# Two edits in a two-block network kernel on one core: 24 one-column sums spread over three weight blocks, and the first group of the retention stage reordered

## The chip, the cores and the metric

The kernel runs on one core of one Trainium2 chip. The metric is device time in microseconds, the median of several executions; a profile of one execution gives a span and every instruction in it. TensorE is called PE here (PEld is its weight load), VectorE DVE, ScalarE ACT, GpSimd POOL, and SP is the engine whose queue issues all transfers.

## The reference

Two models are run one after the other on x, 512 tokens by 1024 features, two layers each.

```python
# first block, layer l of 2
cond = silu(c) @ w_ada[l] + b_ada[l]            # 3 * 1024 columns
shift, scale, gate_raw = split(cond, 3)
h = x * (1 + scale) + shift
proj = h @ w_in[l]                              # HGRN2, RWKV7 and gate columns
...
x = layer_norm(DN_ALPHA * x + (1 + gate_raw) * out, ln_g[l], ln_b[l])

# second block: layer 0 is an RG-LRU mixer, layer 1 is retention
h = rms_norm(x, norm_pre[layer])
o = rglru_mixer(h, ...) if layer == 0 else retention_mixer(h, ...)
x = x + rms_norm(o, norm_post[layer])

# retention: u = h @ w_in gives q, k (4 heads of 256), v and a gate (4 heads of 512)
```

What matters here: in layer 0 of the first block, cond of layer 1 is also computed; and retention starts with x = x + rms_norm(o, norm_post[0]) and a projection of rms_norm(x, norm_pre[1]).

## The kernel before, in words

Activations lie transposed: a tile is 128 features by 512 tokens, and x has eight tiles (KT = 8). All large products go through 231 **weight blocks** of 128 x 1024 numbers (512 KB). Each block passes four stations. SP loads it into one of two slots of w_raw (L552, `load_block`; it waits until POOL has finished with the block before in that slot). ACT copies it to w_hi, rounded (L790, `weights(b)`; it waits for the load and until PE has used block b - 2). POOL subtracts the rounded copy from the raw one in two halves into w_lo (L700). PE multiplies it (L2480, `project`, 24 matmuls of 512 columns: for each of eight tiles high x high, low x high, high x low). Activations are split in the same way into act_hi (ACT) and act_lo (DVE). Every engine has its own hand-written program order, and semaphores tie them together; what stands behind a waiting instruction on its engine waits too.

A **group** (L2499, `side_by_side`) is four blocks interleaved so that four output tiles are built at once, input tile by input tile: step k = 0 to 7 takes 12 matmuls with input tile k, and needs act_hi and act_lo of tile k and one half of the w_lo of block k // 2. After step 1, 3, 5 and 7 a block counts as used.

**Conditioning columns.** In layer 0 of the first block `later_step` on DVE adds up w_ada of layer 1 over the features into `later_acc` (3072 sums per partition), and `condition_next` on PE adds over the partitions: 24 matmuls of one column each (L2576; each shows as two records in the trace). It stands after the fourth of the blocks b_hg, ahead of four kk_sum matmuls in full fp32 (L2625) and the fifth block. `ada_gate` (L2614) is a like piece of 8 columns, four blocks earlier.

**Retention's first group.** RET is the first retention block. DVE runs over the eight tiles of x: it scales the old output by post0 and 1/rms (L1431 into slots_sb), adds it to x (L1428 into area_sb, signals x_done), and makes act_lo of the tile before (L1431 into act_lo_sb). ACT makes act_hi (L1326) and the square (L1191) of each tile. Then DVE adds the eight squares, each add waiting for the one before (L1428 into slots_sb, `add_squares`), and PE sums them over the partitions (L3081, job rms_pre1). In PE's order that sum stands ahead of step 7 of the group. ACT turns it into 1/rms (L810, L812 into const_sb, `inverse_root`), which DVE needs only when it takes the outputs.

SP's order at this place is the following. The change leaves it as it is:

```python
            blocks_to(ret + 4)
            sp.wait_ge(S("x_done"), KT * 3)
            sp.dma_start(x_scr[2].rearrange("k p t -> p k t"), xa[:, :, :]).then_inc(S("x_saved"), 16)
            blocks_to(ret + 5)
            sp.wait_ge(S("x_saved"), 48)
```

So all eight tiles of x must be done before SP issues the save of x (2 MB), and the load of block RET + 4, which PE takes right behind the group, is issued behind that save. ACT's order has `weights(RET + 4)` ahead of `inverse_root`.

Of the kernel before, what the change touches and what calls it, by code (L numbers as in the profile page):

```python
# [21 lines left out]
KT = D // P  # L22
# [157 lines left out]
LATER = [(0, k, 2) for k in range(KT)] + [(1, k, part) for k in range(KT) for part in range(3)]  # L180
# [157 lines left out]
def build(nc, shapes):  # L338
    first, pieces, groups = block_plan()
    jobs = job_plan()  # L340
# [8 lines left out]
    with ExitStack() as ctx:  # L349
# [43 lines left out]
        aux = [ctx.enter_context(nc.psum_tensor(f"aux{i}", [P, T], F32)) for i in range(6)] + proj  # L393
# [12 lines left out]
        def S(name):  # L406

            if name not in made:
                made[name] = sem(name)
            return made[name]  # L410

        RW_LAST = [first["hg", l] - 1 for l in range(DEPTH)]
        SPLITS = {("h", 0): 0, ("hg", 0): 8, ("rw", 0): 12, ("merged", 0): 16, ("h", 1): 24, ("hg", 1): 32,
                  ("rw", 1): 36, ("merged", 1): 40, "lru_h": 48, "lru_y": 56, "ret_h": 68, "ret_y": 76}
# [36 lines left out]
        def job_open(eng, name, turn=0):  # L451

            bank, use = jobs(name, turn)
            wait(eng, aux_read[bank], use)
            return aux[bank][:, :]

        def job_full(ins, name):
            return ins.then_inc(aux_full[jobs(name)[0]], 1)
# [290 lines left out]
        LRU, LRU_OUT, RET, RET_OUT = (first[k, 0] for k in ("lru_in", "lru_out", "ret_in", "ret_out"))  # L749
# [29 lines left out]
        def _(act):  # L779
# [3 lines left out]
            def weights(b, turn=0):  # L783


                if b >= blocks:
                    return
                act.wait_ge(raw_in[b % 2], 16 * (b // 2 + 1) + 32 * turn)
                wait(act, block_used, b - 1 + 4 * turn)
                A(w_hi[:, b % 2, :, :].rearrange("p k n -> p (k n)"), w_raw[:, b % 2, :], ACT.Copy)\  # L790
                    .then_inc(hi_ready, 1)
# [29 lines left out]
            for l in range(DEPTH):  # L821
# [47 lines left out]
                for i in range(4):  # L869
                    x = group_ready(act, ("rw", l, i))  # L870
# [17 lines left out]
                for j in range(QT):  # L888
                    scaled(b + 4 + j, 9 + j)
                    x = job_ready(act, ("w_up", l, j))  # L890
                    job_read(A(P1[:, j, :], x, ACT.Sigmoid, bias=V(f"w0{l}", j)), ("w_up", l, j))
                    x = job_ready(act, ("a_up", l, j))
                    job_read(A(P2[:, j, :], x, ACT.Sigmoid, bias=V(f"a0{l}", j)), ("a_up", l, j))
                for j in range(QT):
                    scaled(b + 8 + j, 13 + j)
                    if l:
                        x = job_ready(act, ("v_up", l, j))
# [102 lines left out]
                for t in range(QT):  # L1000
# [4 lines left out]
                    x = job_ready(act, ("v_turn", l, t))  # L1005
# [19 lines left out]
                    x = job_ready(act, ("k_turn", l, t))  # L1025
# [91 lines left out]
                for j in range(QT):  # L1117
                    x = job_ready(act, ("gn_var", l, j))
# [204 lines left out]
            def ret_high(m):  # L1323

                act.wait_ge(S("x_done"), 2 * KT + m + 1)
                A(act_hi[:, m, :], xa[:, m, :], ACT.Copy, scale=V("pre1", m)).then_inc(split_hi, 1)  # L1326

            for m in range(KT):
                ret_high(m)
                own_square(m, xa[:, m, :])  # L1330
                if m in (4, 7):
                    weights(RET + (m + 5) // 4)
            weights(RET + 4)
            inverse_root(RS_RET, "rms_pre1", 1.0 / D, 1e-6, S("rms_rs"))
            weights(RET + 5)
# [87 lines left out]
        def _(dve):  # L1423
# [3 lines left out]
            def tt(out_ap, a, b, op):  # L1427
                return TT(out_ap, a, b, op)  # L1428
# [18 lines left out]
            def add_squares(key, which):  # L1447

                for m in which:
                    dve.wait_ge(sq_ready, SQUARES[key] + m + 1)  # L1450
                    ins = tt(SQ[:, 0, :], SQ[:, 0, :], SQ[:, m, :], ALU.add)
                    if m == which[-1] and m > 5:
                        ins.then_inc(S("squares_added"), 1)
                    else:
                        chain.done(ins)
# [120 lines left out]
            for l in range(DEPTH):  # L1576
# [14 lines left out]
                for i in range(4):  # L1591
                    dve.wait_ge(S("mu_scaled"), 17 * l + i + 1)
                    x = group_ready(dve, ("rw", l, i))
# [12 lines left out]
                if l == 0:  # L1606
                    x = job_ready(dve, "ada_gate")
# [654 lines left out]
            for m in range(KT + 1):  # L2262
                if m < KT:
                    stt(OUT[:, m, :], OUT[:, m, :], V("post0", m), RS, ALU.mult, ALU.mult).then_inc(S("out_scaled"), 1)
                if m:
                    ret_low(m - 1)
                if m < KT:
                    dve.wait_ge(S("out_scaled"), m + 1)
                    tt(xa[:, m, :], xa[:, m, :], OUT[:, m, :], ALU.add).then_inc(S("x_done"), 1)
            dve.wait_ge(S("x_done"), 3 * KT)  # L2270
            dve.sem_inc(split_src, KT)
            add_squares("pre1", (1, 2, 3, 4, 5, 6, 7))

            def rotate(h, n):

# [182 lines left out]
        def _(pe):  # L2458
# [25 lines left out]
            def side_by_side(name, tiles, fresh=None, steps=None, ready=None):  # L2484

                b = groups[name][0]
                for k, t in enumerate(tiles):
                    if steps and k not in steps:
                        continue
                    s = (b + k // 2) % 2  # L2490
                    if ready:
                        ready(k)
                    pe.wait_ge(lo_ready, 2 * b + k + 1)
                    if fresh is not None:
                        pe.wait_ge(split_lo, fresh + k + 1)
                    for i in range(4):
                        bank = aux[jobs(name + (i,))[0]][:, :] if k else job_open(pe, name + (i,))
                        for n, (w, a) in enumerate(((w_hi, act_hi), (w_hi, act_lo), (w_lo, act_hi))):
                            ins = MM(bank, w[:, s, 4 * (k % 2) + i, :], a[:, t, :], start=(k == 0 and n == 0),  # L2499
                                     stop=(k == len(tiles) - 1 and n == 2))  # L2500
                    if k % 2:
                        used(ins)
# [22 lines left out]
            for l in range(DEPTH):  # L2525
# [40 lines left out]
                    if l == 0 and k == 5:  # L2566
                        condition(3)

                def condition_next():

                    pe.wait_ge(S("later_used"), len(LATER))
                    x = job_open(pe, ("ada", 1, 0))
                    for j in range(24):

                        at = j if j > 15 else 8 * (j % 4 // 2) + 2 * (j // 4) + j % 2
                        ins = MM(x[:, at:at + 1], later_acc[:, P * j:P * j + P], C("ones", 0, 1), start=True, stop=True)  # L2576
                    job_full(ins, ("ada", 1, 0))

                if l == 0:
                    stream(0)  # L2580
# [36 lines left out]

                for m in range(4):
                    used(project(b_hg + m))
                if l == 0:  # L2620
                    condition_next()
                for j in range(QT):
                    x = job_open(pe, ("kk_sum", l, j))
                    pe.wait_ge(S("kk_squares"), 4 * l + j + 1)
# [452 lines left out]
            def added_squares(n, job, last):  # L3077

                x = job_open(pe, job)
                pe.wait_ge(S("squares_added"), n)  # L3080
                ins = MM(x, C("ones"), SQ[:, 0, :], start=True, stop=not last)  # L3081
                if last:
                    pe.wait_ge(sq_ready, last)
                    ins = MM(x, C("ones"), SQ[:, 7, :], start=False, stop=True)
                job_full(ins, job)
# [57 lines left out]
            added_squares(2, "rms_post0", SQUARES["post0"] + 8)  # L3143
            keep_busy(("ret_in", 0, 3), 6)

            def ret_root(k):
                if k == 7:
                    added_squares(3, "rms_pre1", 0)

            def ret_block(h, j):  # L3150
                used(project(RET + 12 * h + j))

# [67 lines left out]
                pe.wait_ge(S("ret_squares"), h + 1)  # L3220
                job_full(MM(x, C("ones"), wa[:, :], start=True, stop=True), ("r_var", h))

            side_by_side(("ret_in", 0), range(KT), fresh=SPLITS["ret_h"], ready=ret_root)
            for j in range(4, 11):
                ret_block(0, j)
            turns(0)
# [76 lines left out]
```

## Time and profile before

| | us |
|---|---|
| median of 3 runs | 1815.9 |
| lowest, highest | 1815.09, 1817.47 |
| profiled execution, its own time | 1817.34 |
| its span | 1815.2 |
| PE busy in it | 1744.2 (96%) |
| DVE, ACT, POOL busy | 1149.7, 826.4, 715.2 |

The profiled execution is 1.4 us longer than the median, and 2.1 us of it lie outside its span. PE is busy in 96% of the span, so the time is made up of PE's instructions, the short waits between them, and the clock at which they run. That clock has two levels, full (2.4 GHz) and half (1.2 GHz); its mean over the execution is 0.992 of full.

### The profile page before, as it was taken

Reading aid. Unit: us, or ns where it says so; the run is one execution under the profiler, and the core shown is the slowest. Engines: PE = TensorE matmul, PEld = TensorE weight load, DVE = VectorE, ACT = ScalarE, POOL = GpSimd, SP = SyncE. Lnnn points to the kernel's source line nnn. Section 1 sums busy time; section 2 is a strip of 40 time slices with the busy share of each in tenths; the row PEclk is TensorE's granted clock in tenths of the full one; section 3 lists DMA queues with packets and bytes.
Section 4 is the critical chain, followed back from the end, with each engine's and each line's share of the span. In section 5 each row is a group of like instructions: output and inputs, shape, how many; then the busy total and the mean of one; then the engine's idle time right before and its main releaser. Section 6 shows DMA issues by size and latency. Waiting matters only on the chain. (4 is left out here: it accounts for less than half of the span.)

```text
span 1815.2 us, 32011 instructions
## 1 busy us (share of the span) xinstructions
PE 1744.2 (96%) x12832; PEld 1378.6 (76%) x12832; DVE 1149.7 (63%) x1535; ACT 826.4 (46%) x1233; POOL 715.2 (39%) x488
## 2 busy tenths in 40 slices
PE   7999999989999999999989999999999999999996
PEld 6777777778786767777788785675777888888875
DVE  6677687776567118787775647788637364636454
ACT  3343655544635333655454626476543333324242
POOL 2555443320253435643410452443544433434342
PEclk9999999999999999999999999999999999999998
DMA  9772222210531522222200524321244212222222
GB/s 368 254 254 96 88 88 98 95 42 4 187 104 58 171 80 82 93 91 93 92 31 29 184 95 165 100 70 58 85 136 140 85 65 82 70 70 82 70 95 103
DMA packets 63187, 193.00 MB, mean 106 GB/s; under 512 B 5936, under 2 KB 6192, under 8 KB 62672
## 3 DMA queue, kind: packets, MB, share of 16 engines
q1 hardware_dynamic: 63056, 191.10, 30.7%
q8 instruction: 101, 1.65, 0.4%
q14 instruction: 30, 0.25, 0.0%
HBM read 173.25 MB, written 17.83 MB: 105 GB/s over the span
## 5 line engine op out<-in xcount | busy, mean ns | idle before, releaser
L700 POOL TENSOR_TENSOR w_lo_sb<-w_raw_sb,w_hi_sb 128x512 fp32r<-128x512 f32 x462 | 690.6, 1516 | 981.9 <-ACT w_hi_sb L790 981.8
L2480 PE MATMUL proj<-act_hi_sb,w_hi_sb 128*128 128x512 f32 x1480 | 600.5, 406 | 8.2 <-DVE area_sb L1428 2.3
L2480 PE MATMUL proj<-act_hi_sb,w_lo_sb 128*128 128x512 f32 x1480 | 577.6, 390 | 0.0
L2480 PE MATMUL proj<-act_lo_sb,w_hi_sb 128*128 128x512 f32 x1480 | 576.4, 389 | 0.0
L790 ACT ACTIVATE w_hi_sb<-w_raw_sb 128x1024 fp32r<-128x1024 f32 x231 | 244.3, 1058 | 648.0 <-PE proj L2480 485.1
L2480 PEld LDWEIGHTS proj<-act_hi_sb,w_hi_sb 128*128 128x128 f32 x1480 | 277.9, 188 | 91.3 <-issue 24.4
L2480 PEld LDWEIGHTS proj<-act_lo_sb,w_hi_sb 128*128 128x128 f32 x1480 | 278.2, 188 | 61.7 <-issue 7.7
L2480 PEld LDWEIGHTS proj<-act_hi_sb,w_lo_sb 128*128 128x128 f32 x1480 | 277.8, 188 | 59.7
L2499 PE MATMUL aux<-act_hi_sb,w_hi_sb 128*128 128x512 f32 x336 | 136.9, 407 | 13.7 <-POOL w_lo_sb L700 5.1
L1428 DVE TENSOR_TENSOR area_sb<-area_sb 128x256 f32<-128x256 f32 (+1 forms) x180 | 118.1, 699 | 44.5 <-PE aux L2667 26.6
L2499 PE MATMUL aux<-act_lo_sb,w_hi_sb 128*128 128x512 f32 x336 | 132.2, 393 | 0.0
L2499 PE MATMUL aux<-act_hi_sb,w_lo_sb 128*128 128x512 f32 x336 | 132.1, 393 | 0.0
L2718 PE MATMUL aux<-area_sb 64*64 64x64 f32 x2944 | 94.9, 226 | 13.9 <-DVE area_sb L1804 7.6
L1428 DVE TENSOR_TENSOR slots_sb<-proj,const_sb 128x512 f32<-128x512 f32 x44 | 30.4, 691 | 118.5 <-PE proj L2480 118.1
L2718 PEld LDWEIGHTS aux<-area_sb 64*64 64x64 f32 x2944 | 86.3, 138 | 21.0 <-DVE area_sb L1804 13.2
L1428 DVE TENSOR_TENSOR slots_sb<-slots_sb 128x512 f32<-128x512 f32 (+1 forms) x71 | 87.6, 1234 | 21.5 <-ACT slots_sb L1191 7.5
L1428 DVE TENSOR_TENSOR area_sb<-area_sb,slots_sb 128x512 f32<-128x512 f32 (+1 forms) x90 | 84.9, 962 | 18.1 <-ACT slots_sb L812 11.3
L2499 PEld LDWEIGHTS aux<-act_hi_sb,w_hi_sb 128*128 128x128 f32 x336 | 63.8, 190 | 35.4 <-POOL w_lo_sb L700 11.7
L1431 DVE SCALAR_TENSOR_TENSOR slots_sb<-proj,derived_sb,stage_sb 128x512 f32<-128x512 f32 x24 | 18.0, 751 | 96.0 <-ACT stage_sb L867 95.9
L2499 PEld LDWEIGHTS aux<-act_lo_sb,w_hi_sb 128*128 128x128 f32 x336 | 64.0, 190 | 14.0 <-issue 1.4
L2499 PEld LDWEIGHTS aux<-act_hi_sb,w_lo_sb 128*128 128x128 f32 x336 | 63.8, 190 | 13.8
L1428 DVE TENSOR_TENSOR slots_sb<-slots_sb,area_sb 128x512 f32<-128x512 f32 (+2 forms) x43 | 50.0, 1177 | 27.9 <-ACT area_sb L921 26.8
(330 smaller groups left out, 2300.5 us busy)
## 6 DMA issues: line engine op xcount, KB each, us to landing
w_raw_sb<-wall SPq DMA_DIRECT2D x231, 512.0 KB, 3.3
area_sb<-w_ada SPq DMA_DIRECT2D x32, 512.0 KB, 5.1
slots_sb<-w_ada SPq DMA_DIRECT2D x32, 256.0 KB, 7.2
gate_scr<-stage_sb SPq DMA_DIRECT2D x32, 256.0 KB, 2.2
area_sb<-gate_scr SPq DMA_DIRECT2D x8, 1024.0 KB, 9.0
x_scr<-area_sb SPq DMA_DIRECT2D x3, 2048.0 KB, 8.0
area_sb<-x_scr SPq DMA_DIRECT2D x2, 2048.0 KB, 13.4
area_sb<-lru_gates SPq DMA_DIRECT2D x1, 3584.0 KB, 11.4
```

The lines of the kernel that those rows point to most:

```text
L700: nc.gpsimd.tensor_tensor(w_lo[:, b % 2, :, :].rearrange("p k n -> p (k n)")[:, half], w_raw[:, b % 2, half], w_hi[:, b % 2, :, :].rearran ...
L790: A(w_hi[:, b % 2, :, :].rearrange("p k n -> p (k n)"), w_raw[:, b % 2, :], ACT.Copy)\
L1428: return TT(out_ap, a, b, op)
L1431: return STT(out=out_ap, in0=in0, scalar=scalar, in1=in1, op0=op0, op1=op1)
L2480: ins = MM(bank, w[:, s, k, :], a[:, t, :], start=(start and i == 0), stop=(stop and i == len(terms) - 1))
L2499: ins = MM(bank, w[:, s, 4 * (k % 2) + i, :], a[:, t, :], start=(k == 0 and n == 0), stop=(k == len(tiles) - 1 and n == 2))
L2718: last.append(MM(x[to, n * j:n * j + n], a(ROWS[q], j), b(ROWS[q], j), start=start and (stop or j == 0), stop=stop and (start or j == QT - ...
```

## The change

Two places of the program are edited.

```diff
@@ ACT, retention's first group
             for m in range(KT):
+                if m in (4, 6):
+                    weights(RET + m // 2)
                 ret_high(m)
                 own_square(m, xa[:, m, :])
-                if m in (4, 7):
-                    weights(RET + (m + 5) // 4)
             weights(RET + 4)
             inverse_root(RS_RET, "rms_pre1", 1.0 / D, 1e-6, S("rms_rs"))
@@ DVE, retention's first group
                     tt(xa[:, m, :], xa[:, m, :], OUT[:, m, :], ALU.add).then_inc(S("x_done"), 1)
+                if 2 < m < KT:
+                    add_squares("pre1", (m - 2,))
             dve.wait_ge(S("x_done"), 3 * KT)
             dve.sem_inc(split_src, KT)
-            add_squares("pre1", (1, 2, 3, 4, 5, 6, 7))
+            add_squares("pre1", (6, 7))
@@ PE, layer 0 of the first block
-                def condition_next():
-
-                    pe.wait_ge(S("later_used"), len(LATER))
-                    x = job_open(pe, ("ada", 1, 0))
-                    for j in range(24):
+                def condition_next(part):
+
+                    if part == 0:
+                        pe.wait_ge(S("later_used"), len(LATER))
+                        x = job_open(pe, ("ada", 1, 0))
+                    else:
+                        x = aux[jobs(("ada", 1, 0))[0]][:, :]
+                    for j in range(8 * part, 8 * part + 8):
...
-                    job_full(ins, ("ada", 1, 0))
+                    if part == 2:
+                        job_full(ins, ("ada", 1, 0))
...
                 for m in range(4):
                     used(project(b_hg + m))
-                if l == 0:
-                    condition_next()
+                    if l == 0 and m:
+                        condition_next(m - 1)
@@ PE, retention's first group
-            def ret_root(k):
-                if k == 7:
-                    added_squares(3, "rms_pre1", 0)
...
-            side_by_side(("ret_in", 0), range(KT), fresh=SPLITS["ret_h"], ready=ret_root)
+            side_by_side(("ret_in", 0), range(KT), fresh=SPLITS["ret_h"])
+            added_squares(3, "rms_pre1", 0)
```

On PE the columns stood in one piece, between the last matmul of block b_hg + 3 and the kk_sum matmuls (const_sb and area_sb are the ones and the sums of `later_acc`). Before:

```order
L2480 MATMUL proj<-act_lo_sb,w_hi_sb 128x512
L2480 MATMUL proj<-act_hi_sb,w_lo_sb 128x512
L2576 MATMUL aux<-const_sb,area_sb 128x1 x24
L2625 MATMUL aux<-area_sb,const_sb 128x512 x4
L2480 MATMUL proj<-act_hi_sb,w_hi_sb 128x512
```

Now, at the same place:

```order
L2482 MATMUL proj<-act_lo_sb,w_hi_sb 128x512
L2482 MATMUL proj<-act_hi_sb,w_lo_sb 128x512
L2581 MATMUL aux<-const_sb,area_sb 128x1 x8
L2631 MATMUL aux<-area_sb,const_sb 128x512 x4
L2482 MATMUL proj<-act_hi_sb,w_hi_sb 128x512
```

The other 16 columns stand in two pieces of 8, each behind the 24 matmuls of a block, b_hg + 1 and b_hg + 2.

On ACT, in retention's first group, a row L1326 is act_hi of a tile, L1191 its square and L790 the conversion of a block. The piece begins with tiles 2 and 3 (the difference shows the moved rows):

```order
 L1191 ACTIVATE slots_sb<-area_sb 128x512
-L1326 ACTIVATE act_hi_sb<-area_sb,vec_sb 128x512
-L1191 ACTIVATE slots_sb<-area_sb 128x512
 L790 ACTIVATE w_hi_sb<-w_raw_sb 128x1024
...
+L790 ACTIVATE w_hi_sb<-w_raw_sb 128x1024
 L1326 ACTIVATE act_hi_sb<-area_sb,vec_sb 128x512
 L1191 ACTIVATE slots_sb<-area_sb 128x512
-L790 ACTIVATE w_hi_sb<-w_raw_sb 128x1024 x2
+L1326 ACTIVATE act_hi_sb<-area_sb,vec_sb 128x512
+L1191 ACTIVATE slots_sb<-area_sb 128x512
+L790 ACTIVATE w_hi_sb<-w_raw_sb 128x1024
 L810 ACT_TABLE_LOAD
```

The conversion of RET + 2 now stands ahead of tile 4 (it stood behind it), that of RET + 3 ahead of tile 6 (it stood behind tile 7), and RET + 4 keeps its place ahead of the root.

On DVE each tile from the fourth on gets one more instruction between its add into x (area_sb) and the next tile's scaling. The end of the loop over tiles:

```order
 L1428 TENSOR_TENSOR area_sb<-area_sb,slots_sb 128x512
+L1428 TENSOR_TENSOR slots_sb<-slots_sb 128x512
 L1431 SCALAR_TENSOR_TENSOR slots_sb<-slots_sb,vec_sb 128x512
 L1431 SCALAR_TENSOR_TENSOR act_lo_sb<-area_sb,vec_sb,act_hi_sb 128x512
 L1428 TENSOR_TENSOR area_sb<-area_sb,slots_sb 128x512
+L1428 TENSOR_TENSOR slots_sb<-slots_sb 128x512
 L1431 SCALAR_TENSOR_TENSOR act_lo_sb<-area_sb,vec_sb,act_hi_sb 128x512
-L1428 TENSOR_TENSOR slots_sb<-slots_sb 128x512 x7
+L1428 TENSOR_TENSOR slots_sb<-slots_sb 128x512 x2
```

Five of the seven adds of squares moved into the loop, four of them ahead of the last tile's add into x, and two stayed behind it. SP and POOL keep their order.

## Rows read from the trace of the kernel before

**Rows 1.** PE's timeline about the columns (start us, duration, line, operands, count)

```profile
143.81 0.39 PE L2480 MATMUL proj<-act_hi_sb,w_lo_sb 128*128 128x512 f32 x1
...
150.59 0.50 PE L2480 MATMUL proj<-act_hi_sb,w_hi_sb 128*128 128x512 f32 x1 [0.21 <-POOL w_lo_sb L700]
...
156.16 6.14 PE L2576 MATMUL aux<-const_sb,area_sb 128*128 128x1 f32 x48
162.17 6.31 PE L2625 MATMUL aux<-area_sb,const_sb 128*128 128x512 f32 x8
167.91 0.80 PE L2480 MATMUL proj<-act_hi_sb,w_hi_sb 128*128 128x512 f32 x1
```

**Rows 2.** PE's timeline at like pieces: 8 columns twice, kk_sum of layer 1

```profile
38.15 1.84 PE L2543 MATMUL aux<-derived_sb,slots_sb 128*128 128x1 f32 x16
...
131.34 1.81 PE L2614 MATMUL aux<-const_sb,area_sb 128*128 128x1 f32 x15
133.02 0.49 PE L2480 MATMUL proj<-act_hi_sb,w_hi_sb 128*128 128x512 f32 x1
...
700.19 3.60 PE L2625 MATMUL aux<-area_sb,const_sb 128*128 128x512 f32 x8
```

**Rows 3.** Windows of 1 us: busy PE, PEld, DVE, ACT, POOL, PE's clock, DMA

```profile
42.00:43.00 1.00, 1.00 (x4) 0.72 (x4) 0.43 (x1) 0.31 (x1) 0.61 (x1) 0.50 1.03 410
133.00:134.00 1.00, 1.00 (x6) 0.85 (x6) 1.00 (x1) 0.00 (x0) 0.35 (x1) 1.00 0.25 102
161.00:162.00 1.00, 1.00 (x7) 1.00 (x6) 0.97 (x2) 0.00 (x0) 0.23 (x1) 0.50 0.01 4
385.00:386.00 1.00, 0.00 (x0) 0.00 (x0) 0.97 (x3) 0.00 (x0) 0.00 (x0) 0.96 0.00 0
389.00:390.00 1.00, 1.00 (x46) 1.00 (x44) 0.00 (x0) 0.57 (x2) 0.00 (x0) 0.83 0.08 16
```

**Rows 4.** DVE's timeline, its first long instruction after the columns

```profile
189.77 2.29 DVE L1428 TENSOR_TENSOR slots_sb<-slots_sb,area_sb 128x2048 f32<-128x2048 f32 x1 [18.64 <-ACT area_sb L921]
```

**Rows 5.** PE's timeline, retention's first group

```profile
1376.61 0.50 PE L2499 MATMUL aux<-act_hi_sb,w_hi_sb 128*128 128x512 f32 x1 [2.67 <-POOL w_lo_sb L700]
...
1381.13 1.10 PE L3081 MATMUL aux<-slots_sb,const_sb 128*128 128x512 f32 x2 [1.50 <-DVE slots_sb L1428]
...
1384.83 0.39 PE L2480 MATMUL proj<-act_hi_sb,w_hi_sb 128*128 128x512 f32 x1
```

**Rows 6.** DVE's timeline in the group, tiles 3, 4 and 6

```profile
1361.39 0.68 DVE L1428 TENSOR_TENSOR area_sb<-area_sb,slots_sb 128x512 f32<-128x512 f32 x1
1361.99 0.75 DVE L1431 SCALAR_TENSOR_TENSOR slots_sb<-slots_sb,vec_sb 128x512 f32<-128x512 f32 x1
1362.87 0.75 DVE L1431 SCALAR_TENSOR_TENSOR act_lo_sb<-area_sb,vec_sb,act_hi_sb 128x512 fp32r<-128x512 f32 x1
1363.54 0.69 DVE L1428 TENSOR_TENSOR area_sb<-area_sb,slots_sb 128x512 f32<-128x512 f32 x1
...
1368.65 1.77 DVE L1428 TENSOR_TENSOR area_sb<-area_sb,slots_sb 128x512 f32<-128x512 f32 x1
```

**Rows 7.** The chain of waits at the adds of squares, in order of time

```profile
1374.75 0.70 DVE slots_sb L1428
...
1375.47 1.64 DVE slots_sb L1428
```

**Rows 8.** Timelines of POOL, ACT and SP's queue about the group

```profile
1366.53 3.35 POOL L700 TENSOR_TENSOR w_lo_sb<-w_raw_sb,w_hi_sb 128x512 fp32r<-128x512 f32 x2 [14.37 <-ACT w_hi_sb L790]
...
1382.78 2.54 POOL L700 TENSOR_TENSOR w_lo_sb<-w_raw_sb,w_hi_sb 128x512 fp32r<-128x512 f32 x2 [4.52 <-ACT w_hi_sb L790]
...
1381.64 1.06 ACT L790 ACTIVATE w_hi_sb<-w_raw_sb 128x1024 fp32r<-128x1024 f32 x1 [6.85 <-DMA w_raw_sb<-wall]
...
1372.60 0.38 SPq L674 DMA_DIRECT2D x_scr<-area_sb  x1
```

**Rows 9.** Block loads from 1340 to 1400 us, from issue to landing

```profile
DMA to landing us min/median/max: 3.2/3.4/8.6
```

## The prediction

> **What bounds the kernel now.** I read the page first: PE is busy for 96% of the span, so what PE executes, at what clock, and the few waits between is the time. Next I read the windows for the clock and PE's timeline at the two places that the change touches. The waits of PE are few and small there, so each can be named.
>
> At the first place PE does not wait, it is slow. From the last matmul of block b_hg + 1, at 143.81, to the first of block b_hg + 4, at 167.91, it takes 24.10 us [rows 1]. In them stand two blocks, the columns (156.16 to 162.17, 6.01 us) and kk_sum (162.17 to 167.91, 5.74 us). The clock is 0.50 in the window from 161 us [rows 3], behind some 5 us in which PE did columns only. The same kk_sum in layer 1, at full clock, has 3.60 us of records against 6.31 [rows 1, 2], so 2.71 us of the 5.74 are the clock's.
>
> At the second place PE waits twice: 2.67 us for POOL ahead of step 6, and 1.50 us for DVE's adds ahead of the sum [rows 5]. What else is late there shows only in ACT's timeline: the conversion of RET + 4 starts at 1381.64, after 6.85 us of waiting for its load [rows 8]. That load is issued behind the save of x, which is issued at 1372.60, right behind the last tile's add. POOL begins 1.14 us after ACT (1382.78) and a half takes 2.54 / 2 = 1.27 us [rows 8], so the first half of w_lo is there at 1384.05, and PE starts RET + 4 at 1384.83 [rows 5]. **This path has only 0.78 us of slack.** It runs: last tile's add, save, load, ACT, POOL, PE; 1372.60 to 1384.05 is 11.45 us.
>
> **Part 1, the columns.** Nothing is removed; the 24 columns stand in three pieces. A piece of 8 is seen at 131.34 to 133.02, 1.68 us [rows 2], with the clock at 1.00 behind it [rows 3]. A block takes 156.16 - 150.59 = 5.57 us [rows 1]. The new stretch: 0.23 (one matmul of 5.57 / 24) + 3 x 1.68 + 2 x 5.57 + 3.03 (kk_sum at full clock, 5.74 - 2.71) = 19.44 us. The gain is 24.10 - 19.44 = **4.7 us**. Of it 2.7 are kk_sum's clock, 1.0 the columns' (6.01 - 5.04), and 1.0 the waits for POOL ahead of the two blocks, the second of 0.21 [rows 1]: a piece of columns now runs in them. Nothing new is waited for. ACT waits for the same complete sums before it converts block b_hg + 2, and that block began at about 144.6 (150.59 less a block and a wait); less 1.14 + 1.27 us for ACT and POOL [rows 8] the sums were complete by 142.2, and part 0 starts at 144.0. Blocks b_hg + 4 and on are needed by PE later than before relative to their conversion, since a conversion follows the block two before. The gain stays: DVE's next long instruction waits 18.64 us for ACT [rows 4], and ACT there waits for PE's blocks, so all engines move up with PE; the transfers behind it are all issued on semaphores of that work. Bounds: at best 5.0, if columns in a full pipeline take a little less; at worst each piece costs the clock (rivals).
>
> **Part 2, PE's side of the group.** The conversion of RET + 3 no longer holds step 6, and the sum no longer holds step 7. Taken alone that would free both waits, 2.67 + 1.50 us. But what comes behind the group is RET + 4, and its path begins with DVE's last add into x.
>
> **Part 2, DVE's side.** A tile takes 1363.54 - 1361.39 = 2.15 us [rows 6]: add, 0.60 later scaling, act_lo, 0.67 later the next add; between scaling and act_lo (0.88) DVE waits for ACT's act_hi. With one more add the wait is covered: 0.60 + 0.72 (a chained add, 1374.75 to 1375.47 [rows 7]) + 0.67 + 0.67 = 2.66 us. Four such tiles lie ahead of the last add: 4 x 0.51 = **2.1 us later**.
>
> Then contention. While POOL converts RET + 2 (3.35 us from 1366.53 instead of 2.54 [rows 8]), DVE's add into x takes 1.77 us instead of 0.69 [rows 6]; when POOL converts RET + 3, an add of squares takes 1.64 instead of 0.70 [rows 7], and so does the one behind it. So one conversion costs a busy DVE two such delays, 2 x 0.95 = 1.9 us. Before, RET + 2 cost this ahead of the last add and RET + 3 cost it behind, among the adds of squares. Now RET + 3 is converted before act_hi of tile 6. Tile 3's add is at 1361.39, tile 5's at 1361.39 + 2 x 2.66 + 1.9 = 1368.6; with the add (0.7), act_hi and square (about 1.3, two ACT instructions of DVE's size) ACT converts RET + 3 at 1370.6 and POOL from 1371.7 to 1375. The last add starts at 1361.39 + 4 x 2.66 + 2 x 1.9 = 1375.8. The whole conversion lies ahead of it: **another 1.9 us later** (at least 0, if POOL hit only idle DVE time, which is gone).
>
> So the save is issued 4.0 us later, at 1376.6, and w_lo is ready for RET + 4 at 1376.6 + 11.45 = 1388.1. PE itself is done sooner: act_lo of tile 6 is ready at about 1375.9, steps 6 and 7 take 2 x 2.78 us, the sum about 0.6, so PE is idle from 1382.1 to 1388.1. RET + 4 starts **3.3 us later** than at 1384.83. The loads of the tables and of RET + 5 move with the save, and PE meets RET + 5 later too (5.6 us after RET + 4), so they add nothing.
>
> A PE idle for 6 us will lose its clock: in the window from 385 us PE was idle and the clock began to fall, and it was back at about 389.3 (the window from 389 shows 0.83 of full) [rows 3]. From 386.0 that is 3.3 us at half speed, 1.6 us of work lost. I take **1.6 us** (bounds 0, if it returns as PE resumes, and 3.3, for twice as long).
>
> On the port there is a rule. The Trainium skill, SBUF — State Buffer, Who interferes with whom, says that DVE and GpSimd share a port pair under an exclusive lock: a DVE instruction with two inputs in SBUF and a GpSimd instruction that reads SBUF block each other for a whole instruction. Here the rows show 0.95 us per half conversion; by the rule it would be a whole half, 1.27 us, and the second conversion would cost 2.5 us instead of 1.9, the sum 0.6 us more. It speaks against moving the conversion among the tiles either way.
>
> **The sum.** -4.7 + 3.3 + 1.6 = **+0.2 us**. Against the profiled execution's own 1817.34 that is 1817.5; it is 1.4 us over the median, so the median forecast is 1815.9 + 0.2 = 1816.1, given as 1816.0. About 0.2%, 3.6 us, is what a measurement of this kernel can tell from no change.
>
> **The rivals.**
> - Load not gated (faster). If the load of RET + 4 landed in the usual 3.4 us [rows 9] and not behind the save, PE would start it at 1376.6 + 0.4 + 3.4 + 1.14 + 1.27 = 1382.8, 2.0 us sooner than before, with no loss of clock: -6.7, 1809.2. Against it: this load took 8.6 [rows 9], and 1372.60 to 1381.64 is that [rows 8]. Chance 0.08.
> - Clock or contention cheaper. The clock costs nothing behind the idle time (-1.4: 1814.5), or RET + 3's conversion does not delay the last add (3.3 becomes 1.4, -1.7: 1814.2). Together 0.22.
> - Dearer by a little: one of the three pieces of columns costs the clock, as the piece at 38.15 seems to have done, with 0.50 at 42 us [rows 2, 3]; 3.4 us at half are 1.7 us: 1817.8. Chance 0.10. The port's full lock, 1816.7, is 0.06.
> - Slower: every piece of columns costs the clock, 3 x 1.7 = 5.1 us, so part 1 gives nothing (+0.4) and part 2 costs 4.9: 1821.2. It decides from two pieces on (+3.6). For it speaks 38.15; against it 131.34, the same number of columns between full blocks, as here. Chance 0.08.
>
> **How the numbers follow.** The main case has 0.46, with 1814.3 to 1818 as its own range. The range over all, 1811.8 to 1819.6, leaves out the load not gated and the clock lost in every piece. Faster by over 0.2% (below 1812.3): 0.08 and a part of the cheaper cases, 0.14. Slower (above 1819.5): 0.08 and a part of the dearer, 0.13. The rest, 0.73, is no difference that can be told.
>
> **What would show it.** After: no window at half clock behind the columns, and kk_sum at 3.0 us; PE's stretch from b_hg + 1's end to b_hg + 4's start 19.4 us. In the group: save issued about 4 us later relative to the group's first matmul; no wait for POOL at step 6 but one for act_lo; ACT waiting for the load until about 1385.6 on the old scale (1381.64 + 4.0); PE waiting about 6 us ahead of RET + 4, with a window at 0.50 behind it. I am wrong if PE goes from the group into RET + 4 without such a wait, or if clocks fall behind the pieces.

## The result, and the profile after

The changed kernel takes 1821.93 us (median of 20 runs), the kernel before, run beside it on the same chip, 1817.9: a ratio of 1.0023, 95% interval 1.0015 to 1.0031, so about 4 us slower (4.0 between the medians, 4.2 by the ratio). I had forecast no measurable difference, +0.2 us. The columns gained nearly what they should. The retention group cost 8.0 us in the profile and not 4.9.

**Where the columns stood.** PE's timeline (start us, duration, line, operands, records):

```profile
142.58 0.39 PE L2482 MATMUL proj<-act_hi_sb,w_lo_sb 128*128 128x512 f32 x1
142.81 1.84 PE L2581 MATMUL aux<-const_sb,area_sb 128*128 128x1 f32 x16
144.51 0.49 PE L2482 MATMUL proj<-act_hi_sb,w_hi_sb 128*128 128x512 f32 x1
...
157.38 1.84 PE L2581 MATMUL aux<-const_sb,area_sb 128*128 128x1 f32 x16
159.08 3.68 PE L2631 MATMUL aux<-area_sb,const_sb 128*128 128x512 f32 x8
...
162.19 0.79 PE L2482 MATMUL proj<-act_hi_sb,w_hi_sb 128*128 128x512 f32 x1
```

From the last matmul of b_hg + 1 to the first of b_hg + 4 it is 162.19 - 142.58 = 19.61 us (forecast 19.44; before 24.10 [rows 1]). A piece of columns takes 1.70 us, and the kk_sum records behind the last take 3.68 instead of 6.31 us.

**The group.** The same view, from the group's first matmul to the block behind the group; in brackets the idle time and who ended it:

```profile
1352.62 0.47 PE L2501 MATMUL aux<-act_hi_sb,w_hi_sb 128*128 128x512 f32 x1 [0.85 <-issue]
1364.28 0.47 PE L2501 MATMUL aux<-act_hi_sb,w_hi_sb 128*128 128x512 f32 x1 [0.50 <-DVE act_lo_sb L1431]
1371.59 0.47 PE L2501 MATMUL aux<-act_hi_sb,w_hi_sb 128*128 128x512 f32 x1 [1.60 <-DVE act_lo_sb L1431]
1377.12 1.02 PE L3087 MATMUL aux<-slots_sb,const_sb 128*128 128x512 f32 x2
1385.39 0.80 PE L2482 MATMUL proj<-act_hi_sb,w_hi_sb 128*128 128x512 f32 x1 [7.25 <-POOL w_lo_sb L700]
```

Both old waits [rows 5] are gone, POOL's ahead of step 6 and DVE's ahead of the sum. Two short ones for DVE's act_lo have come (0.50 and 1.60 us), and in place of the old ones stands one of 7.25 us ahead of RET + 4. RET + 4 starts 32.77 us behind the group's first matmul; in the kernel before, whose group began at 1357.28, it was 27.55. I use this measure, time behind the group's first matmul, in all kernels below, since they reach the group at different times.

**DVE and ACT.** DVE's timeline, tiles 6 and 7:

```profile
1367.31 1.78 DVE L1428 TENSOR_TENSOR slots_sb<-slots_sb 128x512 f32<-128x512 f32 x1
1369.12 1.66 DVE L1431 SCALAR_TENSOR_TENSOR slots_sb<-slots_sb,vec_sb 128x512 f32<-128x512 f32 x1
1370.71 0.74 DVE L1431 SCALAR_TENSOR_TENSOR act_lo_sb<-area_sb,vec_sb,act_hi_sb 128x512 fp32r<-128x512 f32 x1
1371.37 0.68 DVE L1428 TENSOR_TENSOR area_sb<-area_sb,slots_sb 128x512 f32<-128x512 f32 x1
```

The first two rows are the contention with POOL's conversion of RET + 3, ahead of the last add into x. SP's queue and ACT:

```profile
1372.08 0.38 SPq L674 DMA_DIRECT2D x_scr<-area_sb  x1
1372.51 0.57 SPq L552 DMA_DIRECT2D w_raw_sb<-wall  x1
```

```profile
1382.95 1.06 ACT L790 ACTIVATE w_hi_sb<-w_raw_sb 128x1024 fp32r<-128x1024 f32 x1 [9.62 <-DMA w_raw_sb<-wall]
```

The save is issued 19.46 us behind the group's start (15.32 before): 4.14 us later, forecast 4.0. But ACT begins RET + 4 at 10.87 us behind the save; in [rows 8] it was 9.04. That was not forecast.

**The clock.** Windows of 1 us: busy PE, PEld, DVE, ACT, POOL, PE's clock, DMA.

```profile
161.00:162.00 1.00, 1.00 (x4) 0.45 (x3) 0.99 (x1) 0.00 (x0) 0.44 (x1) 1.00 0.00 0
1380.00:1381.00 1.00, 0.00 (x0) 0.00 (x0) 0.00 (x0) 0.00 (x0) 0.00 (x0) 0.94 1.07 291
1381.00:1382.00 1.00, 0.00 (x0) 0.00 (x0) 0.00 (x0) 0.00 (x0) 0.00 (x0) 0.50 0.60 172
1390.00:1391.00 1.00, 1.00 (x4) 0.81 (x3) 0.37 (x1) 0.00 (x0) 1.00 (x2) 0.50 0.00 0
1391.00:1392.00 1.00, 1.00 (x5) 0.77 (x5) 0.00 (x0) 0.00 (x0) 0.39 (x1) 0.94 0.00 0
```

Behind the columns the clock is full. PE idles from 1378.1, the clock falls at about 1380.9, and it is back at about 1391.1 (the window from 1391 shows 0.94), so PE works for 1391.1 - 1385.4 = 5.7 us at half: 2.9 us lost, forecast 1.6. In the profile of the kernel before, the clock stays full all through the group and behind it.

**The books of the retention part.** The save 4.14, the landing 1.83, less the slack of 0.78, make 5.19 us; measured 5.22. With the clock's 2.9 it is 8.1. The trace says 8.0: the changed kernel is 4.66 us ahead at the group's start, and 3.3 behind at the end. That the 4.66 looks so much like my 4.7 is partly luck. Eight kernels here are the same up to the group (the changed one and all but those of experiments 2 and 5), and in their profiles it begins anywhere from 1350.07 to 1355.47 us. The stretch itself, 24.10 against 19.61 us, is the better measure of the columns.

### The profile page after: what moved, and what is told of

The parts are those of the page before. It is cut to its first block, busy times and chain, and to the rows that moved or that the text cites. A ratio compares the mean times of both kernels' runs of the same rounds, so it can differ in the third digit from the quotient of the medians.

```text
span 1818.5 us, 32007 instructions
## 1 busy us (share of the span) xinstructions
PE 1742.2 (96%) x12832; PEld 1378.7 (76%) x12832; DVE 1148.0 (63%) x1535; ACT 826.9 (45%) x1233; POOL 715.0 (39%) x488
## 4 chain that ended last, share of the span: by engine, by line
PE 48%; issue 33%; POOL 14%; DVE 3%; ACT 1%; POOLq 0%; ACTq 0%; DVEq 0%
PE proj L2482 35%; POOL w_lo_sb L700 14%; PE aux L2724 3%; PE aux L2672 1%; PE aux L2512 1%; PE aux L3205 1%; PE aux L3211 1%; DVE area_sb L1428 1%; PE aux L3202 1%; PE proj L2724 1%; PE aux L2705 0%; DVE area_sb L1804 0%; PE aux L2670 0%; PE aux L2694 0%; PE aux L2714 0%
## 5 line engine op out<-in xcount | busy, mean ns | idle before, releaser
L790 ACT ACTIVATE w_hi_sb<-w_raw_sb 128x1024 fp32r<-128x1024 f32 x231 | 244.3, 1057 | 648.6 <-PE proj L2482 482.0
L1428 DVE TENSOR_TENSOR slots_sb<-proj,const_sb 128x512 f32<-128x512 f32 x44 | 30.4, 690 | 120.5 <-PE proj L2482 120.2
```

## The experiments

**1 and 2: each part alone.** The first kernel has PE's columns in three pieces and nothing else; the second only the retention group's edits.

> The conditioning columns in three pieces, retention's group as before. Theory (the columns gave what was forecast, the loss is all in retention's group): the stretch from b_hg + 1's end to b_hg + 4's start takes 19.5 us instead of 23.9, and the time is 4.4 us under the kernel before (ratio 0.9976). Rival (the half clock behind the columns was an accident of the one profiled execution of before, and the columns give nothing on average): ratio 1.000.

> Retention's group as changed, the columns in one piece as before. Theory: PE waits about 7 us for w_lo of RET + 4 behind the group, then runs at half clock, and the time is 8 us over the kernel before (ratio 1.0045). Rival (the columns gave nothing on average): 4 us over (ratio 1.0023), the whole measured difference.

Measured: columns alone 1811.76 us, ratio 0.9977 (0.9966 to 0.9988), -4.2 us. Retention alone 1823.69 us, ratio 1.0045 (1.0029 to 1.0062), +8.2 us. They add up to the whole, +4.0. The half clock behind the columns was no accident of one execution: the profiles of all three kernels with the columns in one piece have it (before, experiments 2 and 5), and none of those with three pieces. The save of the second comes at 19.46 us, ACT's conversion 10.73 us behind it, and PE starts RET + 4 at 32.64 us:

```profile
1391.19 0.79 PE L2482 MATMUL proj<-act_hi_sb,w_hi_sb 128*128 128x512 f32 x1 [7.11 <-POOL w_lo_sb L700]
```

So all of the loss is the retention edits', and the columns' price per piece, the rival that would have ended slower, is not there.

The first kernel shows one thing more. Its group is that of the kernel before, with the same wait of 2.67 us ahead of step 6, but here the clock falls, at about 1372.0, and is back at about 1375.4:

```profile
1373.00:1374.00 1.00, 1.00 (x4) 0.81 (x3) 0.96 (x2) 0.00 (x0) 0.00 (x0) 0.50 0.95 221
```

RET + 4 still starts at 27.65 us (27.55 before), since the slower step only fills the wait for the sum. So one and the same wait left the clock full in one profile and halved it in another.

**3: the loads of RET + 4 and RET + 5 ahead of the save**, in the changed kernel. If the late save does its harm only through the load behind it, the harm must go.

```diff
-            blocks_to(ret + 4)
+            blocks_to(ret + 6)
             sp.wait_ge(S("x_done"), KT * 3)
             sp.dma_start(x_scr[2].rearrange("k p t -> p k t"), xa[:, :, :]).then_inc(S("x_saved"), 16)
-            blocks_to(ret + 5)
```

> The changed kernel, but SP issues the loads of blocks RET + 4 and RET + 5 ahead of its wait for x and of the save of x. Theory (the load behind the save is what PE waits for): the wait ahead of RET + 4 goes, and the half clock with it: 7.2 + 2.8 = 10 us less than the changed kernel, about 6 us under the kernel before (ratio 0.997); RS_RET and the tables may then be late next and give back up to 3 us. Rival (the group is slower in itself, by DVE's extra adds and POOL's port): at most 3 us of the loss goes, ratio 1.000 or more.

Measured: 1810.2 us, ratio 0.997 (0.9959 to 0.9981). The save is as late as ever (19.46), but PE goes through. All of PE's waits in its timeline, then the sum and RET + 4 (no bracket, no wait):

```profile
1363.42 0.47 PE L2500 MATMUL aux<-act_hi_sb,w_hi_sb 128*128 128x512 f32 x1 [0.53 <-DVE act_lo_sb L1430]
1370.74 0.47 PE L2500 MATMUL aux<-act_hi_sb,w_hi_sb 128*128 128x512 f32 x1 [1.57 <-DVE act_lo_sb L1430]
1376.27 1.02 PE L3086 MATMUL aux<-slots_sb,const_sb 128*128 128x512 f32 x2
1376.73 0.80 PE L2481 MATMUL proj<-act_hi_sb,w_hi_sb 128*128 128x512 f32 x1
```

RET + 4 starts at 24.96 us, 7.8 sooner than in the changed kernel, and the clock stays full. The place of the load in SP's queue is the cause. This version beats both kernels. Most of its lead over the kernel before is that of the columns: against them alone (1811.76 us, same chip) it is 1.6 us lower in the median, and the two ratios' intervals overlap.

**4: PE kept busy while it waits.** Eight fp32 matmuls on constants, 16 records (`keep_busy`, used elsewhere in the kernel), stand behind the sum of the changed kernel; the wait stays, only the clock is kept.

```diff
             added_squares(3, "rms_pre1", 0)
+            keep_busy(("rk_turn", 0, 0), 8)
```

> The changed kernel, with 8 dummy fp32 matmuls (some 6.9 us, results unused) behind the sum of squares, in PE's wait. Theory (the idle time costs the clock, and the clock is a term of its own): PE starts RET + 4 at the same time relative to the group, no window at half clock follows, and 2.8 us are gained over the changed kernel (about 1.5 us over the kernel before, ratio 1.0007). Rival (the clock's share is small, or the dummies delay RET + 4): within 1 us of the changed kernel, ratio 1.0018 to 1.003.

Measured: 1817.08 us, ratio 1.0007 (0.9995 to 1.0019), against 1.0023 for the changed kernel: 0.16%, 2.9 us, is the clock's share. The intervals of the two ratios leave that between nearly nothing and some 5 us; the profiles, counted from the group's first matmul to the end, differ by 2.5. RET + 4 starts at 32.90 us, as late as before the edit, and the clock is 1.00 in the window where it had been half:

```profile
1375.75 7.03 PE L2535 MATMUL aux<-const_sb 128*128 128x512 f32 x16
1383.28 0.50 PE L2482 MATMUL proj<-act_hi_sb,w_hi_sb 128*128 128x512 f32 x1 [0.50 <-POOL w_lo_sb L700]
```

```profile
1383.00:1384.00 1.00, 0.72 (x3) 0.64 (x4) 0.00 (x0) 0.97 (x3) 1.00 (x2) 1.00 0.06 16
```

**5: the loads first, in the kernel before.** Is the gain of experiment 3 that of SP's order by itself? Its edit is the same, made in the kernel before.

> The kernel before with one edit: SP issues the loads of RET + 4 and RET + 5 ahead of the wait for x and of the save, as in e3. The theory says that in the kernel before PE hardly waits for that load (its path had 0.78 us of slack), so that the change of the order gives next to nothing by itself: RET + 4 starts in PE where it did relative to the group's first matmul, 27.5 us behind it, within 0.3 us; ratio to before 1.000 (0.9985 to 1.001). The rival says that the gain of e3 is that of SP's order and not of the late save made harmless: then it is seen here too, as a ratio of 0.997 or so.

Measured: 1818.12 us, ratio 1.0013 (1.0000 to 1.0025). The rival is out, but my number for the place was wrong: RET + 4 starts at 32.37 us and not 27.5. With its load early, POOL converts RET + 3 and RET + 4 without a pause, both over DVE's adds of squares, and PE waits for the sum. The save is late too, 21.71 us behind the group's first matmul, since SP must issue RET + 5 first and its slot comes free only with RET + 3's conversion. Timelines of DVE, POOL and PE:

```profile
1372.14 8.86 DVE L1427 TENSOR_TENSOR slots_sb<-slots_sb 128x512 f32<-128x512 f32 x7
```

```profile
1372.98 6.75 POOL L699 TENSOR_TENSOR w_lo_sb<-w_raw_sb,w_hi_sb 128x512 fp32r<-128x512 f32 x4 [5.00 <-ACT w_hi_sb L789]
```

```profile
1374.72 0.50 PE L2498 MATMUL aux<-act_hi_sb,w_hi_sb 128*128 128x512 f32 x1 [2.65 <-POOL w_lo_sb L699]
...
1381.14 2.05 PE L3080 MATMUL aux<-slots_sb,const_sb 128*128 128x512 f32 x2 [3.36 <-DVE slots_sb L1427]
```

The sum starts 25.76 us behind the group's first matmul, 1.9 us later than before. The other 2.9 us are the clock's, which falls at about 1380.5 in the wait and is back at about 1387.3, so that the sum and step 7 take 6.61 us instead of 3.70:

```profile
1386.00:1387.00 1.00, 1.00 (x4) 0.81 (x3) 0.00 (x0) 0.00 (x0) 0.00 (x0) 0.50 0.48 66
```

This one execution is 2.1 us over its kernel's median, so the others need not all lose as much. SP's order by itself pays nothing; it pays in a kernel whose other edits keep the sum and the conversions out of its way. Which of them it needs is looked at again in experiment 8.

**6 and 7: the two halves of DVE's lateness.** One is the changed kernel with the seven adds behind the tiles again, the other with RET + 3 converted behind tile 7 again.

```diff
# 6, DVE
-                if 2 < m < KT:
-                    add_squares("pre1", (m - 2,))
...
-            add_squares("pre1", (6, 7))
+            add_squares("pre1", (1, 2, 3, 4, 5, 6, 7))
# 7, ACT
-                if m in (4, 6):
-                    weights(RET + m // 2)
+                if m == 4:
+                    weights(RET + 2)
                 ret_high(m)
                 own_square(m, xa[:, m, :])
+                if m == 7:
+                    weights(RET + 3)
```

> The changed kernel with the adds of squares all behind the tiles on DVE, as they were before; ACT's order, PE's order and the columns are the changed ones. By the theory the four chained adds ahead of the last add into x are 2.1 of the 4.1 us by which the save came late: the save is issued at 17.4 us behind the group's first matmul (before 15.3, changed 19.5), RET + 4 starts 2 us sooner than in the changed kernel, at 30.7 us, and PE's idle time is shorter by as much or less, since the sum of squares is later. Ratio to before about 1.001. The rival, that the moved conversion of RET + 3 is what holds DVE, has the save still at 19 us or later and the ratio at 1.002.

> The changed kernel with the conversion of RET + 3 behind tile 7 on ACT, as it was before; everything else is the changed kernel. By the theory the conversion among the tiles is 1.9 to 2.0 of the 4.1 us: the save is issued at 17.5 us behind the group's first matmul, the waits of PE for w_lo of RET + 3 come back at step 6 (2 to 3 us, covered by the idle time that is there anyway), RET + 4 starts at about 30.8 us. Ratio to before about 1.001. If the two edits on DVE's path overlap instead of adding up, the save here is at 18.5 us or later and so it is in the twin kernel. The landing of RET + 4's load behind the save took 1.8 us longer in both kernels that have the retention edit than in both that don't: if it is the POOL's conversion at the time of the save that makes the difference, it is back to 9.0 us here; if it is DVE's adds, it is so in the twin.

Measured, behind the group's first matmul:

| | before | 6: squares behind | 7: RET + 3 behind | changed |
|---|---|---|---|---|
| save issued | 15.32 | 17.24 | 17.44 | 19.46 |
| ACT's RET + 4, behind the save | 9.04 | 9.01 | 9.01 | 10.87 |
| RET + 4 in PE | 27.55 | 28.70 | 29.78 | 32.77 |
| PE's work at half clock behind its last long wait | 0 | 6.0 | 4.7 | 5.7 |
| ratio | | 1.0002 (0.9991 to 1.0012) | 0.9995 (0.9986 to 1.0003) | 1.0023 |

Each edit costs the save what I gave it: 19.46 - 17.24 = 2.22 us for the adds (forecast 2.1), 19.46 - 17.44 = 2.02 for the conversion (1.9), and they add up. The ratios are 0.8 and 1.5 thousandths better than I expected of them. In kernel 6 the landing is back at 9.0 us, which I had counted at 10.9. In kernel 7 it is too, but there PE waits elsewhere, at step 6, 4.16 us for POOL's w_lo of RET + 3:

```profile
1372.97 0.80 PE L2503 MATMUL aux<-act_hi_sb,w_hi_sb 128*128 128x512 f32 x1 [4.16 <-POOL w_lo_sb L700]
```

```profile
1373.00:1374.00 1.00, 1.00 (x3) 0.81 (x4) 0.00 (x0) 0.00 (x0) 1.00 (x1) 0.50 1.05 379
```

Behind that wait the clock is at half until about 1377.7, and steps 6 and 7 take 7.79 us instead of 5.53, so in kernel 7 it is this wait and the clock that place RET + 4, no longer the landing. In kernel 6 two shorter waits (1.85 us for the sum, 3.36 for RET + 4) cost the clock as well, 6.0 us at half behind the start of RET + 4 and so 3.0 lost. Its 1.15 us of later start and these 3.0, less the columns' 4.2, make about nothing, and its ratio is 1.0002.

The landing follows neither edit: with either of them undone it is short.

**8: experiment 3 with the squares behind the tiles**, to remove its last wait, 1.57 us ahead of step 6. The edit is that of 6, made in 3.

> The kernel with the loads of RET + 4 and RET + 5 ahead of the save (e3), and the adds of squares all behind the tiles. In e3 PE still waited 1.6 us ahead of step 6 for act_lo, which DVE makes late. By the theory act_lo comes 1.5 to 2 us sooner here and that wait goes; the sum of squares comes later (some 2 us), and PE waits for it behind the group, 0.5 to 1.5 us. So RET + 4 starts between 24.0 and 25.0 us behind the group's first matmul (24.96 in e3), ratio to before 0.9965 (0.9955 to 0.998). The rival says the sum behind the group takes back all, or more, so the ratio is 0.998 or over.

Measured: 1812.47 us, ratio 0.9982 (0.9972 to 0.9991); RET + 4 at 26.31 us. The wait at step 6 did go. The one for the sum is 3.77 us instead of the 0.5 to 1.5 expected, because POOL's conversion of RET + 4 now lies over the adds:

```profile
1375.85 1.10 PE L3084 MATMUL aux<-slots_sb,const_sb 128*128 128x512 f32 x2 [3.77 <-DVE slots_sb L1427]
```

```profile
1368.74 6.97 DVE L1427 TENSOR_TENSOR slots_sb<-slots_sb 128x512 f32<-128x512 f32 x7
```

The rival had the mechanism and the ratio. The clock stays full behind this wait. Experiment 3 keeps the lowest ratio, though the two intervals overlap. Kernels 6 and 8 differ in SP's order alone, and the order brings 1.0002 down to 0.9982. So it pays with the squares behind the tiles too. What kernels 3 and 8 share, and kernel 5 lacks, are the columns in pieces, the earlier conversions and the sum behind the group; no run takes these apart.

**9: why the load landed late.** In the changed kernel SP now waits for RET + 4's landing before it issues the tables, whose packets could compete with the load's last ones.

```diff
+            sp.wait_ge(raw_in[(ret + 4) % 2], 16 * ((ret + 4) // 2 + 1))
             sp.dma_start(xa[:, 0:4, :].rearrange("p a t -> p (a t)"), dram["tables"]).then_inc(S("tables_in"), 16)
```

> The changed kernel, in which SP waits for the landing of RET + 4's load before it issues the tables (1 MB in packets of 8 KB), which are issued 7.73 us behind the save otherwise. In the three kernels whose RET + 4 came late, ACT begins its conversion 10.7 to 11.0 us behind the save instead of 9.0; in their records three or four of the load's 128 packets of 4 KB come among packets of the tables, 0.6 to 1.8 us behind the rest, and a packet of instructions (16 KB, 0.97 us) was fetched just ahead. If the fetch holds one of the 16 DMA engines and the tables' packets then take turns with what is left of the load, the load without the tables lands 0.5 us sooner: ACT begins at 10.2 to 10.5 us behind the save, RET + 4 in PE at 32.2 us behind the group's first matmul, ratio to before 1.002. If the fetch alone makes it, 10.87 stays; if the tables alone, 9.0 to 9.2 and RET + 4 at 31.0, ratio 1.001. The tables come 2 us later, which may make DVE late where it needs them.

Measured: 1819.14 us, ratio 1.0018 (1.0006 to 1.003). ACT begins 10.68 us behind the save, against 10.87 and my 10.2 to 10.5; RET + 4 starts at 32.60 us. The tables are not it. What is seen are the DMA counts of short windows. A load is 128 packets of 4 KB, and tables have packets of 8 KB, so that the load's packets are those under 8 KB and not under 512 B. Kernel before, 8.6 to 10.6 us behind the save, when its load has landed (2 small, 2 under 8 KB, so none of 4 KB):

```profile
DMA packets 66, 0.52 MB, mean 262 GB/s; under 512 B 2, under 2 KB 2, under 8 KB 2
```

Changed kernel, 1380.50 to 1380.70, and then, in the second fence, 1380.68 to 1382.68 (8.6 to 10.6 behind its save):

```profile
DMA packets 16, 0.02 MB, mean 123 GB/s; under 512 B 13, under 2 KB 13, under 8 KB 15
...
q8 instruction: 1, 0.02, 30.4%
```

```profile
DMA packets 67, 0.52 MB, mean 260 GB/s; under 512 B 2, under 2 KB 2, under 8 KB 5
```

A packet of instructions is fetched as the load ends, and three packets of the load come after all others. The last experiment, from 8.8 to 10.9 us behind its save, without the tables: three load packets and one small one, alone, on 16 engines.

```profile
DMA packets 4, 0.01 MB, mean 6 GB/s; under 512 B 1, under 2 KB 1, under 8 KB 4
```

So traffic of other transfers does not hold them. The kernels with retention alone and with PE kept busy show the same (under 512 B 2 and 4, under 8 KB 5 and 8). The times tie them to the instruction packet. In the changed kernel it starts at 1380.59 and lasts 0.97 us (30.4% of 16 engines in 0.2 us), so it ends at 1381.56. The first of the three load packets starts at 1381.55, alone in the window from 1381.50 to 1381.60:

```profile
DMA packets 1, 0.00 MB, mean 41 GB/s; under 512 B 0, under 2 KB 0, under 8 KB 1
```

In the other three late kernels (experiments 2, 4 and 9) a load packet starts within 0.02 us of the end of the instruction packet in the same way. Kernel 6 has such a packet too (window 1381.0 to 1381.3), yet no load packet comes after 8.6 us:

```profile
DMA packets 64, 0.52 MB, mean 258 GB/s; under 512 B 1, under 2 KB 1, under 8 KB 1
```

There it starts 8.54 us behind the save, later than in any of the four (8.35 to 8.51), when the last load packet has started (8.46). It ends at 1382.23, and what starts then is a packet of the tables, alone in the window from 1382.15 to 1382.30:

```profile
DMA packets 1, 0.01 MB, mean 55 GB/s; under 512 B 0, under 2 KB 0, under 8 KB 0
```

In kernel 7 the instruction packet starts at 8.84 us, behind the whole load, and in the kernel before and in kernel 1 there is none at this time. In all four of these ACT begins 9.0 us behind the save. So in eight kernels the landing is late exactly where an instruction packet starts ahead of the load's last packets. I still argue this from the order of events: no view names the DMA engine of a packet, and no experiment moved the fetch.

## Why the prediction was wrong, point by point

- **The columns: right.** Stretch 19.61 us for 19.44; no lost clock behind any piece; alone -4.2 us (-6.2 to -2.2) for -4.7. The rivals that charged a clock loss to one or all pieces are out.
- **The save 4.0 us later: right**, 4.14, with both halves measured apart, 2.22 and 2.02.
- **PE's old waits go, one ahead of RET + 4 comes: right**, and moving the load removes it (experiment 3). The rival "load not gated" is out: its ratio is what one gets by changing SP's order.
- **Failed: "w_lo is ready for RET + 4 at 1376.6 + 11.45".** I carried the path from the save to w_lo over whole, with a transfer in it whose landing was read once. From the save to ACT's start it took 10.87 us instead of 9.04, 1.83 us more (1.6 to 2.0 in the four kernels with both retention edits and the load behind the save), and RET + 4 started 5.2 and not 3.3 us later. The tables are excluded. The instruction packet is what the times point at, an argument and not a test; what makes the fetch fall there stays open.
- **Failed: "I take 1.6 us" for the clock.** The mechanism was right; the size was 2.9 us, inside my bounds of 0 to 3.3. I had read the return from one stretch, at 389. With nearly the same idle time (7.11 us) retention alone was at half until about 1394.5, 3.3 us of work and so 1.7 lost, kernel 9 (7.06 us) for 5.0, and the changed kernel (7.25) for 5.7. One row does not give that number.
- **The sum.** -4.7 + 3.3 + 1.6 became, in the profile, -4.7 + 5.2 + 2.9 = +3.4, and the span is 3.3 longer. The two failures both point the same way, 3.2 us, and that is the miss against the kernel before. No rival combined a late landing with a dear clock, so the range ended at 1819.6, too low. With twenty executions of each kernel the interval excludes no change, so my likeliest outcome, no difference that can be told (0.73), did not come. The forecast time of 1816.0 missed by more, 5.9 us, and 2.0 of them are its base: I added to 1815.9, the median of three executions, and the median of twenty is 1817.9. That the rival with a clock loss in every piece had 1821.2 is chance, for its mechanism did not occur.
- **The port.** Forecast 0.95 us per half conversion; the exclusive lock would be 1.27. Seven adds of squares in a row take 5.04 us (timeline of kernel 6) when POOL is idle, 6.97 with one conversion over them and 8.86 with two. A conversion costs DVE 1.93 and 1.89 us, about 0.95 per half. POOL in turn takes 3.35 us and not 2.54 [rows 8]. The rule of the Trainium skill (SBUF — State Buffer, Who interferes with whom), read as a block of DVE for a whole POOL instruction, overstates the cost here, and the measurement decides. By it a conversion would cost DVE 2.5 us, an estimate from POOL's 2.54.

```profile
1374.14 5.04 DVE L1428 TENSOR_TENSOR slots_sb<-slots_sb 128x512 f32<-128x512 f32 x7
```

## What to carry to other kernels

A wait removed on the busy engine is worth only what the next late thing leaves. Here that was a load queued behind a save that waits for DVE's last add, so work moved onto DVE ahead of that add paid in full, and moving the load ahead of the save (two lines of SP's order) turned +0.23% into -0.3%, of which the columns alone are -0.23%. Give a transfer on the path a range and not one landing time, and when a wait may cost the clock, count the loss to its upper bound: the same 2.67 us of waiting cost it in one profile and not in another. Before two conversions or long adds are moved, lay POOL's and DVE's rows over each other: the same adds cost 5.0, 7.0 or 8.9 us by how many conversions lie over them.

## What the runs showed of the hardware that was not expected

- The same 2 MB save and the 512 KB load behind it, issued 0.43 us apart, took 9.0 or 10.7 to 11.0 us from save to ACT's start, by kernel, in one profile of each. The difference sits in the last three or four packets of the load. The first of them starts within 0.02 us of the end of a packet of instructions (16 KB, 0.97 us), and they come late even with the DMA engines otherwise idle (experiment 9).
- Three waits of PE of like length (7.25, 7.11 and 7.06 us) left it at half clock for 5.7, 3.3 and 5.0 us of work.
- The clock fell in a wait of 3.36 us (kernel 5) and stayed full through one of 3.77 us (kernel 8).
